# When layer 1's weight sums are made, and the order of the plain heads on two engines

## The chip, the core and the metric

The kernel runs on one core of a Trainium2 chip. The metric is the device time of one execution in microseconds (us). The kernel before was run three times: median 1727.48 us, from 1726.52 to 1728.12.

## The reference

Two layers over 512 prompt positions and 64 sample positions, all in float32 (D = 1024, 8 heads, feed-forward width 4096). Each layer:

```python
h = rmsnorm(x, g_pre_mix)
z = h @ w_in                       # [B | C | xin | c_q | c_kv | k_rope | gate_conv | gate_mla]
y_a = B * short_conv(C * xin)      # causal, 3 taps, with the last two rows kept
y_b = mla_attention(...)           # latent attention, chunk-causal mask, rotary key; the
                                   # sample attends to 512 cached positions and its own
merged = sigmoid(gate_conv) * y_a + sigmoid(gate_mla) * y_b
x = x + rmsnorm(merged @ w_o, g_post_mix)
f = square(relu(rmsnorm(x, g_pre_ffn) @ w1)) @ w2
x = x + rmsnorm(f, g_post_ffn)
```

The outputs are the two x, and for each layer the new latents, rotary keys and convolution rows.

## The kernel before, in words

**Arithmetic.** Every product of two float32 matrices is made of three products of fp32r matrices: each operand is split in a high part (a cast by ScalarE, `..._hi`) and a low part (a subtraction by VectorE, `..._lo`), and TensorE adds low x high, high x low and high x high in one PSUM bank (`mm3`, lines 811 to 813). So each weight block (128 x 1024, 512 KB) is loaded by SP into a slot, cast by ScalarE, subtracted by VectorE, and only then multiplied. Columns are worked on in two halves of 288 positions. Results of 288 columns go through a ring of four PSUM banks (`ring`), whose banks ScalarE and VectorE free by reading them (`ring_full`, `ring_free`); four more banks (`att`) serve attention and the second matrix of the feed-forward.

**Order.** All five instruction streams are written out by hand, each engine in its own order, with semaphores between them. SP issues nearly all loads, each after a wait for the product that last used the slot (`ring_full`, `w2_full`). An engine that waits holds up all that stands behind it in its stream.

**Stages of a layer.** First the latents' projection. Then eight heads. Heads 0, 1 and 7 are plain: five blocks (the two gates, C, xin, B), with the query, key and value projections, the scores, the turning of the probabilities and the product of probabilities and values between them. TensorE's order in a plain head is: block 0, projections, block 1, scores, block 2, turns, block 3, `attended` (probabilities x values), block 4. Heads 2 to 6 are mixed: two pairs of blocks each are multiplied by seven half products instead of eight, with sums and differences of the weight blocks (`weight_sums`) and of the inputs (`turn`). Then the output projection with the sample's attention in it, and the feed-forward in eight groups. Groups 0 and 1 are plain; groups 2 to 7 use the same seven products for two pairs of blocks (p = 0, 1) each. In their steady part TensorE alternates between a pair's seven ring products and eight banks of the second matrix (`w2_blocks`, 4 `att` banks in turn). I call one such pair with its eight banks a half group.

**The weight sums of the mixed heads.** There are 20, ten for each layer (2 for each of 5 mixed heads; `N_SUMS` = 20, `MIXED` = 5). GpSimd makes them in DRAM, by DMAs alone: three copies (`sums_copy`, lines 1129 to 1131, 1 MB), two accumulating DMAs (`sums_add_first`, 1135 and 1136), and two more (`sums_add_second`, 1139; `sums_add_third`, 1142), 256 KB each. `sums_steps` runs them as a pipeline: in step n it waits for the landing of what came before, copies sum n + 1, and adds to sums n, n - 1 and n - 2. The first two steps run before layer 0's key rotation (also on GpSimd), all others right behind it, for both layers in one go. SP loads the finished sums for the mixed heads (line 949 for 512 KB, 954 for halves) after waiting for `sums_third`. In the feed-forward's pairs the sums are made in SBUF by VectorE instead (`pair_sums`, lines 3009 to 3014), after it has waited for the landing of both blocks of the pair.

**A plain head on the two engines.** In ScalarE's stream (line 1501 on) the exponents are followed by `next_weight(2)` (the cast of a block of the next head), `small_hi(L, h + 1)` (the cast of the next head's small weights, which waits for their DMA) and `turned_hi(h)` (the casts of the turned probabilities, line 1494). VectorE has `next_weight(2)`, for head 1 `head_mix(3)` (2477), `turned_lo(h)`, `small_lo(h + 1)`, then the convolution: `u` from the banks of block 3 (2567 to 2570), ScalarE's `conv_begin`, `conv_taps`, the gate product, a weight, `attention_out` (2453, 2454), `gated_out` and `merge` (2355, 2363).

**Head 7** also prepares the sample's attention: casts of the transposed cache (`cth`, `kch`), copies of the new latents behind it, and the cache in natural order (`nah`, line 1567), with VectorE's `cache_lo(0)`, `(1)`, `(2)`. Right behind head 7 stands the output projection: `merged_lo` (2744) gives the low parts of the eight merged rows; rows 0 to 6 come back from DRAM, row 7 is head 7's own. TensorE starts it with rows 0 to 3 of output columns 0 to 3, then `s_scores(0)`, rows 4 to 7, and `s_turn(0)` (3663), which needs the sample's softmax (2777).

**The feed-forward's loads.** SP loads a pair's first block when product 1 of the pair before is done, its second after product 4 (`after_pair`, `pair_load`), and the blocks of the second matrix after the banks that used the slot (`after_w2`). VectorE's order for a half group (`outs_and_lo`) is: `pair_sums`, then the reads of the second matrix's banks (`w2_out`, 2923) with the low parts of the next pair between them:

```python
pair_sums(g1, p1)
f_done(g0, p0, 2)
w2_out(g, k0)
f_done(g0, p0, 3)
w2_out(g, k0 + 1)
```

## Time and profile before

| | before |
|---|---|
| median of 3 runs | 1727.48 us (1726.52 to 1728.12) |
| the profiled execution | 1726.3 us, its span 1724.5 us |
| TensorE busy | 1705.7 us (99%) |
| VectorE busy | 1309.3 us (76%) |
| ScalarE busy | 855.1 us (50%) |
| GpSimd busy | 122.3 us (7%) |
| granted TensorE clock, mean | 0.997 |
| SP's DMA queue | 185.45 MB, 33.5% of 16 engines |
| GpSimd's DMA queue | 41.95 MB, 13.8% of 16 engines |

The span runs from the first to the last instruction of the program; the profiled execution's own time has 1.8 us around it. Engines: PE is TensorE, PEld its weight loads, DVE VectorE, ACT ScalarE, POOL GpSimd, SP the queue that issues loads; a q behind an engine's name is its sequencer. L with a number is a line of the kernel. Most low parts are made in one helper, line 2071, so they are told apart by the tiles named. In a timeline's row the brackets at the end give the idle time of the engine before the instruction, and what ended it. Weight loads are `w_raw<-blocks_in`, issued at line 859 when a whole block is loaded.

### The profile page before, as it was taken

What the parts mean: (1) busy time and instruction counts of PE and PEld (TensorE: products, weight loads), DVE (VectorE), ACT (ScalarE), POOL (GpSimd) and SP (SyncE); (2) the same over time, 40 slices, a digit from 0 to 9 for tenths busy, and PEclk for the clock granted to TensorE, in tenths of its full rate; (3) what the DMA queues carried; (4) which work ended last, traced back from release to release, by engine and by line L of the source; (5) the groups of instructions that cost most, each with busy time, mean ns of one, the idle gap of its engine ahead of it and who ended that gap; (6) DMA issues with size and microseconds to landing.
All of it is one profiled execution on the core that took longest, in us unless ns stands there. A gap on an engine that the chain in (4) does not pass through costs nothing.

```text
span 1724.5 us, 31894 instructions
## 1 busy us (share of the span) xinstructions
PE 1705.7 (99%) x12735; PEld 1690.9 (98%) x12735; DVE 1309.3 (76%) x2514; ACT 855.1 (50%) x1665; POOL 122.3 (7%) x163
## 2 busy tenths in 40 slices
PE   9999999999999999999999999999999999999997
PEld 9998999999999999999999999999999999999997
DVE  7788787767798786668687797777678887777665
ACT  7625454545465454436366364545435536444452
POOL 1412121212210000000001000000000000000000
PEclk9999999999999999999999999999999999999998
DMA  7899898898762232323124454343532213322231
GB/s 239 198 212 244 214 209 211 178 249 235 163 129 97 89 96 86 99 86 111 60 84 149 148 166 139 114 121 112 171 117 98 99 37 111 98 86 87 74 99 55
DMA packets 90996, 231.54 MB, mean 134 GB/s; under 512 B 9824, under 2 KB 25440, under 8 KB 90848
## 3 DMA queue, kind: packets, MB, share of 16 engines
q1 hardware_dynamic: 71968, 185.45, 33.5%
q0 software_dynamic: 17600, 41.95, 13.8%
q8 instruction: 101, 1.65, 0.4%
q10 hardware_dynamic: 1280, 2.10, 0.3%
q14 instruction: 47, 0.39, 0.1%
HBM read 214.39 MB, written 57.02 MB: 157 GB/s over the span
## 4 chain that ended last, share of the span: by engine, by line
PE 94%; DMA 2%; DVE 2%; ACT 1%; SPq 1%; issue 0%; DVEq 0%; ACTq 0%
PE ring L811 19%; PE ring L813 19%; PE ring L812 19%; PE att L811 11%; PE att L813 11%; PE att L812 11%; PE att L3527 1%; DMA cache_pe_raw<-cache_pe_in 1%; PE att L806 1%; PE att L805 1%; DMA small_raw<-small_in 1%; DMA xs_lo_raw<-h_kept 1%; PE att L818 0%; ACT rope_s L1291 0%; PE att L3343 0%
## 5 line engine op out<-in xcount | busy, mean ns | idle before, releaser
L811 PE MATMUL ring<-xs_hi,w_lo 128*128 128x288 f32 x1872 | 556.6, 297 | 4.3 <-DVE xs_lo L2744 2.2
L813 PE MATMUL ring<-xs_hi,w_hi 128*128 128x288 f32 x1872 | 551.4, 295 | 0.0
L812 PE MATMUL ring<-xs_lo,w_hi 128*128 128x288 f32 x1872 | 551.3, 294 | 0.0
L2071 DVE TENSOR_TENSOR w_lo<-w_raw,w_hi 128x1024 fp32r<-128x1024 f32 (+1 forms) x364 | 370.0, 1035 | 37.3 <-ACT w_hi L1220 27.2
L811 PEld LDWEIGHTS ring<-xs_hi,w_lo 128*128 128x128 f32 x1872 | 351.6, 188 | 7.3 <-DVE ga L2355 2.4
L812 PEld LDWEIGHTS ring<-xs_lo,w_hi 128*128 128x128 f32 x1872 | 351.7, 188 | 1.4
L813 PEld LDWEIGHTS ring<-xs_hi,w_hi 128*128 128x128 f32 x1872 | 351.5, 188 | 0.0
L813 PE MATMUL att<-f_hi,w_hi 128*128 128x288 f32 x960 | 283.2, 295 | 0.0
L812 PE MATMUL att<-f_lo,w_hi 128*128 128x288 f32 x960 | 282.9, 295 | 0.0
L811 PE MATMUL att<-f_hi,w_lo 128*128 128x288 f32 x960 | 282.6, 294 | 0.0
L811 PEld LDWEIGHTS att<-f_hi,w_lo 128*128 128x128 f32 x960 | 180.4, 188 | 0.0
L812 PEld LDWEIGHTS att<-f_lo,w_hi 128*128 128x128 f32 x960 | 180.4, 188 | 0.0
L813 PEld LDWEIGHTS att<-f_hi,w_hi 128*128 128x128 f32 x960 | 180.4, 188 | 0.0
L1212 ACT ACTIVATE w_hi<-w_raw 128x1024 fp32r<-128x1024 f32 x98 | 101.9, 1053 | 87.0 <-DMA w_raw<-blocks_in 86.8
L1220 ACT ACTIVATE w_hi<-w_raw 128x1024 fp32r<-128x1024 f32 x118 | 122.8, 1051 | 7.2 <-DMA w_raw<-blocks_in 6.5
L2923 DVE TENSOR_TENSOR my<-att,my 128x288 f32<-128x288 f32 x160 | 70.8, 451 | 67.7 <-PE att L813 67.7
L813 PE MATMUL ring<-mix_hi,w_hi 128*128 128x288 f32 x384 | 113.5, 295 | 0.0
L811 PE MATMUL ring<-mix_hi,w_lo 128*128 128x288 f32 x384 | 113.1, 295 | 0.0
L812 PE MATMUL ring<-mix_lo,w_hi 128*128 128x288 f32 x360 | 105.9, 294 | 0.0
L811 PE MATMUL ring<-turn_hi,w_lo 128*128 128x288 f32 x320 | 94.9, 296 | 0.0
L812 PE MATMUL ring<-turn_lo,w_hi 128*128 128x288 f32 x320 | 94.4, 295 | 0.0
L813 PE MATMUL ring<-turn_hi,w_hi 128*128 128x288 f32 x320 | 94.2, 295 | 0.0
(342 smaller groups left out, 3184.4 us busy)
## 6 DMA issues: line engine op xcount, KB each, us to landing
w_raw<-blocks_in SPq DMA_DIRECT2D x195, 512.0 KB, 3.7
weight_sums<-blocks_in POOLq DMA_DIRECT2D x80, 256.0 KB, 7.2
w_raw<-blocks_in SPq DMA_DIRECT2D x62, 256.0 KB, 4.6
weight_sums<-blocks_in POOLq DMA_DIRECT2D x20, 512.0 KB, 5.6
weight_sums<-weight_sums POOLq DMA_DIRECT2D x40, 256.0 KB, 7.6
w_raw<-weight_sums SPq DMA_DIRECT2D x20, 512.0 KB, 4.6
w_raw<-weight_sums SPq DMA_DIRECT2D x40, 256.0 KB, 4.4
small_raw<-small_in SPq DMA_DIRECT2D x16, 320.0 KB, 4.6
```

Source lines behind the costliest of these rows:

```text
L805: pe.matmul(out, both, keys[1], start=False, stop=False)
L806: return pe.matmul(out, both, keys[0], start=False, stop=True)
L811: pe.matmul(out, w[1], x[0], start=first, stop=False)
L812: pe.matmul(out, w[0], x[1], start=False, stop=False)
L813: return pe.matmul(out, w[0], x[0], start=False, stop=last)
L1212: act.activation(hi, raw, ACT.Copy).then_inc(pl.weights_hi, 1)
L1220: act.activation(hi, raw, ACT.Copy).then_inc(pl.weights_hi, 1)
L2071: return dve.tensor_tensor(out, a, hi.bitcast(F32), ALU.subtract)
L2923: dve.tensor_tensor(dst, src, dst, ALU.add).then_inc(pl.w2_free, 1)
L3527: last = pe.transpose(att[:, to:to + P], pl.probs[:, PO[t] + P * j:PO[t] + P * (j + 1)], ident)
```

## The change

It has four parts. On GpSimd, `sums_steps` gets a first and an end sum, and layer 1's ten sums are made in a second run of the pipeline. That run starts after layer 0's are complete and the first product of pair (2, 1) of layer 0's feed-forward is full. In plain heads `turned_hi` goes ahead of `next_weight(2)` and `small_hi` on ScalarE, and `turned_lo` ahead of `next_weight(2)` on VectorE. In head 7 the copies of the new latents come after `conv_begin`, `cache_lo(1)` after the products into `u`, and the cast and subtraction of the natural cache go behind head 7, after the weight block `wo` 4. At the output projection `merged_lo` of rows 0 to 6 comes before head 7's `gated_out` and `merge`. No instruction is added or removed, but for the waits of the second run.

```diff
@@ -1141,24 +1141,24 @@
         def sums_add_third(n):
             pool.dma_start(pl.sums[n][:, 3, :], pl.sums[n][:, 0, :], accum_op=ALU.add).then_inc(pl.sums_third, 16)
 
-        def sums_steps(n0, n1):
+        def sums_steps(n0, n1, first, end):
 
             for n in range(n0, n1):
-                if n < N_SUMS:
+                if n < end:
                     pool.wait_ge(pl.sums_copied, 48 * (n + 1))
-                if 1 <= n <= N_SUMS:
+                if first < n <= end:
                     pool.wait_ge(pl.sums_first, 32 * n)
-                if 2 <= n <= N_SUMS + 1:
+                if first + 1 < n <= end + 1:
                     pool.wait_ge(pl.sums_second, 16 * (n - 1))
-                if n >= 3:
+                if n > first + 2:
                     pool.wait_ge(pl.sums_third, 16 * (n - 2))
-                if n + 1 < N_SUMS:
+                if n + 1 < end:
                     sums_copy(n + 1)
-                if n < N_SUMS:
+                if n < end:
                     sums_add_first(n)
-                if 1 <= n <= N_SUMS:
+                if first < n <= end:
                     sums_add_second(n - 1)
-                if n >= 2:
+                if n > first + 1:
                     sums_add_third(n - 2)
 
         pool.sem_inc(pl.ring_free, 4)
@@ -1186,13 +1186,17 @@
 
         pool.wait_ge(pl.x_landed[7], 16)
         sums_copy(0)
-        sums_steps(0, BEFORE_KEYS)
+        sums_steps(0, BEFORE_KEYS, 0, 2 * MIXED)
         for L in range(DEPTH):
             pool.wait_ge(pl.tables_landed, L * 32 + 32)
             key_rope(L, 0)
             key_rope(L, 1)
             if L == 0:
-                sums_steps(BEFORE_KEYS, N_SUMS + 2)
+                sums_steps(BEFORE_KEYS, 2 * MIXED + 2, 0, 2 * MIXED)
+                pool.wait_ge(pl.sums_third, 16 * 2 * MIXED)
+                pool.wait_ge(pl.ring_full, full(0, r_pair(2, 1, 0)))
+                sums_copy(2 * MIXED)
+                sums_steps(2 * MIXED, N_SUMS + 2, 2 * MIXED, N_SUMS)
         for i, (m0, m1) in enumerate(TAIL_MOVED):
             pool.wait_ge(pl.tail_factored, i + 1)
             nc.gpsimd.tensor_tensor(pl.x[:, m0:m1, cols(1)], pl.x[:, m0:m1, cols(1)], pl.last[:, m0:m1, :], ALU.add) \
@@ -1547,14 +1551,18 @@
                 next_weight(1)
                 absorbed_hi(h)
                 exponents(h)
+                turned_hi(h)
                 next_weight(2)
                 small_hi(L, h + 1)
-                turned_hi(h)
 
                 if h == HEADS - 1:
                     eng.wait_ge(pl.cache_landed, L * 48 + 48)
                     act.activation(pl.cth[:, :, 0:PAST], pl.ctraw[:, :, 0:PAST], ACT.Copy).then_inc(pl.cache_hi, 1)
                     act.activation(pl.kch[:, 0:PAST], pl.kcraw[:, 0:PAST], ACT.Copy).then_inc(pl.cache_hi, 1)
+                eng.wait_ge(pl.ring_free, ring_freed(3, 1))
+                apart()
+                conv_begin(h)
+                if h == HEADS - 1:
                     eng.wait_ge(pl.latent_lo, L * 4 + 4)
                     eng.wait_ge(pl.key_lo, L * 2 + 2)
                     apart()
@@ -1563,11 +1571,6 @@
                     for to, src in ((pl.kch, pl.keh), (pl.kcl, pl.kel)):
                         ins = act.activation(to[:, PAST:NT], src[:, NP_:NT].bitcast(F32), ACT.Copy)
                     ins.then_inc(pl.cache_new, 1)
-                    eng.wait_ge(pl.nat_landed, L * 16 + 16)
-                    act.activation(pl.nah[:, :, :], pl.naraw[:, :, :], ACT.Copy).then_inc(pl.cache_hi, 1)
-                eng.wait_ge(pl.ring_free, ring_freed(3, 1))
-                apart()
-                conv_begin(h)
                 next_weight(3)
                 if h == FIRST_MIXED - 1:
                     eng.wait_ge(pl.turn_made, 4 * (L + 1))
@@ -1665,6 +1668,8 @@
             for k in range(HEADS):
                 x_hi_a(k)
             weight_hi(L, n_wo(4), SLOT_WO[4], use_wo(4))
+            eng.wait_ge(pl.nat_landed, L * 16 + 16)
+            act.activation(pl.nah[:, :, :], pl.naraw[:, :, :], ACT.Copy).then_inc(pl.cache_hi, 1)
             eng.dma_start(conv_out[L], pl.conv_tail[:, :, :]).then_inc(pl.conv_stored, 16)
             eng.wait_ge(pl.new_turned, L + 1)
             act.activation(pl.n4h[:, :], pl.att[:, 1536:1792], ACT.Copy).then_inc(pl.cache_hi, 1)
@@ -2544,8 +2549,6 @@
                 if first:
                     pos_lo(L, 3)
                 head_out(h, pl.cv[:, cols(1)], 2, 1, pl.rx2)
-                if not first:
-                    next_weight(2)
                 if h == FIRST_MIXED - 1:
                     head_mix(3)
 
@@ -2553,13 +2556,11 @@
                 if first:
                     next_weight(0)
                     next_weight(1)
-                    next_weight(2)
+                next_weight(2)
                 small_lo(h + 1)
 
                 if h == HEADS - 1:
                     cache_lo(0, pl.ctl[:, :, 0:PAST], pl.ctraw[:, :, 0:PAST], pl.cth[:, :, 0:PAST])
-                    cache_lo(1, pl.kcl[:, 0:PAST], pl.kcraw[:, 0:PAST], pl.kch[:, 0:PAST])
-                    cache_lo(2, pl.nal[:, :, :], pl.naraw[:, :, :], pl.nah[:, :, :])
 
                 conv_state(h)
                 own_ring(h, 2, 1)
@@ -2569,6 +2570,8 @@
                 dve.tensor_tensor(pl.u[:, 2 + NH:2 + NP_], src[:, 0:NP_ - NH], pl.cv[:, NH:NP_], ALU.mult)
                 dve.tensor_tensor(pl.u[:, 4 + NP_:4 + NT], src[:, NP_ - NH:NH], pl.cv[:, NP_:NT], ALU.mult) \
                     .then_inc(pl.ring_free, 1)
+                if h == HEADS - 1:
+                    cache_lo(1, pl.kcl[:, 0:PAST], pl.kcraw[:, 0:PAST], pl.kch[:, 0:PAST])
                 conv_taps(h)
 
                 dve.scalar_tensor_tensor(out=pl.ga[:, 0:NP_], in0=pl.ga[:, 0:NP_], scalar=1.0,
@@ -2745,12 +2748,12 @@
                                          in1=pl.xh[:, m, t].bitcast(F32), op0=ALU.mult, op1=ALU.subtract) \
                     .then_inc(pl.x_lo, 1)
 
+            for k in range(HEADS - 1):
+                merged_lo(x_part(L, X_WOA + k), k, cols(0))
             k = HEADS - 1
             gated_out(k, 0)
             own_ring(k, 4, 0)
             merge(k, slice(0, NH), pl.merged_a)
-            for k in range(HEADS - 1):
-                merged_lo(x_part(L, X_WOA + k), k, cols(0))
             weight_lo(L, n_wo(3), SLOT_WO[3])
             k = HEADS - 1
             gated_out(k, 1)
@@ -2759,6 +2762,7 @@
             merge(k, slice(NH, NP_), pl.merged)
 
             weight_lo(L, n_wo(4), SLOT_WO[4])
+            cache_lo(2, pl.nal[:, :, :], pl.naraw[:, :, :], pl.nah[:, :, :])
             cache_lo(3, pl.n4l[:, :], pl.att[:, 1536:1792], pl.n4h[:, :])
             for k in range(HEADS):
                 merged_lo(x_part(L, X_WOB + k), k, slice(NH, NP_))
```

## Rows read from the trace of the kernel before

**Rows 1.** The page, part 1: busy us (share of the span) and instructions.

```profile
PE 1705.7 (99%) x12735; PEld 1690.9 (98%) x12735; DVE 1309.3 (76%) x2514; ACT 855.1 (50%) x1665; POOL 122.3 (7%) x163
```

**Rows 2.** TensorE's waits: what waited, releaser, us in total, times, longest.

```profile
PE att L811 <- DVE probs_t_lo L2071: 2.4, 1, 2.4
PE ring L811 <- DVE xs_lo L2744: 2.2, 1, 2.2
...
PE att L811 <- DVE k_lo L2071: 0.7, 1, 0.7
...
PE att L811 <- DVE rx L2454: 0.6, 1, 0.6
```

**Rows 3.** The timeline of GpSimd: start us, us, engine, line, operation; idle before it in brackets.

```profile
214.87 0.75 POOL L1129 DMA_DIRECT2D weight_sums<-blocks_in  x1 [7.08 <-DMA weight_sums<-weight_sums]
...
248.27 1.13 POOL L1139 DMA_DIRECT2D weight_sums<-weight_sums  x1
...
439.31 0.76 POOL L1129 DMA_DIRECT2D weight_sums<-blocks_in  x1 [4.42 <-DMA weight_sums<-weight_sums]
...
446.30 0.85 POOL L1136 DMA_DIRECT2D weight_sums<-blocks_in  x1 [4.28 <-issue]
...
453.64 0.81 POOL L1142 DMA_DIRECT2D weight_sums<-weight_sums  x1 [5.65 <-issue]
458.75 0.75 POOL L1129 DMA_DIRECT2D weight_sums<-blocks_in  x1 [4.30 <-DMA weight_sums<-weight_sums]
```

**Rows 4.** Busy us by stretch: PE, PEld, DVE, ACT, POOL, PEclk, DMA share, GB/s.

```profile
591.00:790.00 199.00, 199.00 (x1505) 199.00 (x1504) 142.91 (x266) 94.92 (x187) 0.00 (x0) 1.00 0.30 91
```

**Rows 5.** Timeline around head 1's turned probabilities, layer 0, three engines.

```profile
132.58 1.70 ACT L1228 ACTIVATE small_hi<-small_raw 128x1792 fp32r<-128x1792 f32 x1 [6.94 <-DMA small_raw<-small_in]
...
134.80 1.62 DVE L2071 TENSOR_TENSOR probs_t_lo<-att,probs_t_hi 128x512 fp32r<-128x512 f32 x3 [5.32 <-ACT probs_t_hi L1494]
...
136.47 0.50 PE L811 MATMUL att<-probs_t_hi,v_lo 128*128 128x512 f32 x1 [2.44 <-DVE probs_t_lo L2071]
```

**Rows 6.** Timeline of head 7 and the output projection, layer 0, VectorE and TensorE.

```profile
394.04 1.23 DVE L2071 TENSOR_TENSOR cache_n_lo<-cache_n_raw,cache_n_hi 128x1024 fp32r<-128x1024 f32 x1 [0.34 <-ACT cache_n_hi L1567]
...
401.94 0.46 DVE L2363 TENSOR_TENSOR my<-my,ga 128x288 f32<-128x288 f32 x1
402.32 2.66 DVE L2744 SCALAR_TENSOR_TENSOR xs_lo<-my,xs_hi 128x288 fp32r<-128x288 f32 x7
...
413.77 0.52 DVE L2777 TENSOR_SCALAR probs_s<-probs_s,stat_s 128x576 f32<-128x576 f32 x1
...
417.75 0.60 PE L3663 MATMUL att<-consts,probs_s 128*128 128x128 f32 x4
```

**Rows 7.** Timeline of ScalarE: it reads the first product of pair (2, 1).

```profile
590.97 0.39 ACT L1839 ACTIVATE pair_u<-ring 128x288 f32<-128x288 f32 x1
```

**Rows 8.** VectorE's block sums, 600 to 790 us: ns min/median/max, first and last start.

```profile
L3009 DVE TENSOR_TENSOR w_raw<-w_raw x8: 683/692/694, 613.1 to 778.9; 128x512 f32<-128x512 f32 x8
```

**Rows 9.** Weight loads of SP, 600 to 790 us: from issue to landing.

```profile
DMA to landing us min/median/max: 3.4/3.5/5.0
```

**Rows 10.** Timeline of one half group of the feed-forward, VectorE and TensorE.

```profile
683.56 0.69 DVE L3009 TENSOR_TENSOR w_raw<-w_raw 128x512 f32<-128x512 f32 x1
...
686.47 0.45 DVE L2923 TENSOR_TENSOR my<-att,my 128x288 f32<-128x288 f32 x1
...
689.27 0.30 PE L811 MATMUL att<-f_hi,w_lo 128*128 128x288 f32 x1
```

**Rows 11.** The same loads in layer 0's heads, 160 to 380 us.

```profile
DMA to landing us min/median/max: 3.6/7.9/11.3
```

**Rows 12.** DMAs issued from 249.0 to 249.9 us: count, KB, us to landing.

```profile
w_raw<-blocks_in SPq DMA_DIRECT2D x1, 512.0 KB, 8.4
weight_sums<-weight_sums POOLq DMA_DIRECT2D x1, 256.0 KB, 8.2
```

**Rows 13.** SP's loads of stored sums, 900 to 1100 us: first and last start.

```profile
L949 SPq DMA_DIRECT2D w_raw<-weight_sums x6: 320/324/339, 971.9 to 1088.1; - x6
```

## The prediction

> **What bounds the kernel now.** I read the page's busy times first [rows 1]: TensorE works 1705.7 of the 1724.5 us of the span, so everything that any reordering can win lies in the 18.8 us left, of which a part is start and end. The list of TensorE's own waits [rows 2] says where: 2.4 us in layer 0 before head 1's product of probabilities and values (it waits for the turned probabilities' low parts), 2.2 us in layer 0 before the output projection (it waits for the first low part of the merged rows), 0.6 and 0.7 us just behind the first of these, at head 2's keys and query. What is left is under 1 us each or belongs to the start and the end. Both large waits stand in layer 0 only; layer 1 runs the same code without them. What layer 0 has and layer 1 has not is GpSimd's traffic: the block sums of both layers are made by its DMAs, the twentieth copied at 458.75 us [rows 3]. From 591 to 790 us, in the feed-forward, TensorE has no idle time at all (199.00 of 199.00) and the DMA engines are 0.30 busy [rows 4]. So the change removes at most 2.4 + 2.2 = 4.6 us, and moves a load on the DMA engines into a stretch that has been free of waits. Hence the question is what that stretch can bear.
>
> **Head 1's turned probabilities.** ScalarE stood 6.94 us before the cast of the small weights, until their DMA landed at 132.6 us, and only then split the turned probabilities, which had long been there; VectorE waited 5.32 us with it, and TensorE came 2.44 us late at 136.47 [rows 5]. In the new order the split goes ahead of that wait and of one weight cast on each engine. VectorE is then free at 129.5 us (134.80 less its idle 5.32), its three subtractions take 1.62 us, so they are done near 131.1, ahead of 134.0, when TensorE asks. The 2.4 us go. What is late next: the small weights land as before, since no DMA of SP's queue moves. VectorE takes them at about 134.3 instead of 136.3, when its three subtractions ended: 2.0 us earlier, where TensorE comes 2.4 earlier; the wait of 0.6 us at head 2's keys, which hangs on VectorE, grows by 0.4. Behind it head 2 waits for rows reloaded by DMA. Those loads are issued when TensorE finishes a product, so they move up with it, but they queue behind GpSimd's transfers, which don't. That gives back between 0 and 2.0 us; I take 0.4, since TensorE's waits on that chain are 0.7 us and less. Saved: 2.4 - 0.4 - 0.4 = 1.6 us, with 0 and 2.4 as ends. Heads 0 and 7, and layer 1, have no such wait, so there the order is worth nothing, and the weight cast that now comes second has a whole head of cover: its block is multiplied in the next head.
>
> **Head 7.** In layer 0 the natural cache's subtraction (1.23 us) ran before the convolution, and behind it the weight, gating and merge steps of VectorE held the seven merged rows' subtractions back to 402.32 us; TensorE had then been ready since 400.7 [rows 2, 6]. The change takes the 1.23 us from in front, and puts the seven (2.66 us, so 0.38 each) before the gating and the merging (some 0.4 us each, [rows 6]) that only the eighth row needs. With 1.2 + 0.8 us out of the way the first low part is there at 402.32 + 0.38 - 2.0 = 400.7, just where TensorE asks: the 2.2 us go, with 1.4 as the low end if the high parts on ScalarE hold it. The moved cast and subtraction (1.05 us, as ScalarE's casts of this size, and 1.23) now precede the sample's first softmax: its normalisation ended at 414.29 and TensorE turned it at 417.75 [rows 6], so 3.4 us of cover for at most 2.3 us; without that cover it would cost up to 2.3. I take 0.
>
> **The sums, on the side that gets lighter.** Layer 0's ten end near 275 us instead of sharing the queue with the other ten until after 458. From there to 591 us the loads come faster, but TensorE waits there only before the output projection, counted already: 0.
>
> **The sums, on the side that gets heavier.** The new wait on GpSimd ends with the first product of group 2's second pair, read at 590.97 us [rows 7]. Ten copies lie between 214.87 and 458.75, 24.4 us each beside the heads' traffic, and the last two 19.4 apart [rows 3]; so the ten run from 591 to about 820 us. They meet eight half groups, from 613.1 to 778.9 us, counted by VectorE's block sums, 23.7 us apart [rows 8]. Nothing is queued behind the wait on GpSimd but the sums and the next layer's key rotation, some 80 us after they end.
> In each half group two weight blocks land just in time; loads of the stretch land in 3.5 us (3.4 to 5.0, [rows 9]). Upon the second one VectorE's block sum starts at 683.56, with no idle time before it, and behind it, in order, the first read of a second-matrix bank ends at 686.92; TensorE wants that bank at 689.27 [rows 10]. The spare is 2.35 us, so a landing time above 3.5 + 2.3 = 5.8 us stops TensorE by the excess.
> In layer 0's heads, beside the sums, such loads took 7.9 us in the median and up to 11.3 [rows 11]. One that met the sums almost alone, issued behind an accumulation of 248.27, took 8.4 us, and its GpSimd neighbour 8.2 [rows 3, 12]: a load seems to wait for what GpSimd has outstanding, and lands about 1.2 us behind it. With little else running, one cycle of the sums shows three waits of 7.0, 7.3 and 5.1 us (439.31, 446.30, 453.64, 458.75, [rows 3]). A load issued x us into a wait of T lands T - x + 1.2 us later and is too late by T - x - 4.6. Averaged over the cycle: (2.4^2 + 2.7^2 + 0.5^2) / 2 / 19.4 = 0.34 us per half group, 2.7 us for eight. The weight loads lengthen those waits by their own work, some 1.3 us each; then it is (3.7^2 + 4.0^2 + 1.8^2) / 2 / 23.3 = 0.70 us, 5.6 us for eight. These bound the likely case; I take 5.2, close to the second, since four loads in each half group meet the sums. Outer ends: 0 if the loads get their share at once, and 8 x (8.4 - 5.8) = 21 us if every one is hit like the one of rows 12.
> The Trainium skill, page "DMA: Bandwidth & Descriptors", section "Queues, rings and completion order", says that each DMA engine takes turns between the queues it has work for, packet by packet. By that alone a load would wait for one packet of GpSimd's and no more, and the term would be near 0 instead of 5.2. The row of 8.4 us speaks against it, though it is one load.
>
> **Sum.** -1.6 - 2.2 + 5.2 = +1.4 us on the profiled execution of 1726.3 us, which is 1.2 us below the median of the runs. On the median: 1727.5 + 1.4 = 1728.9 us.
>
> **Rivals.** All differ from the forecast in layer 0's feed-forward. A measurement of this kernel tells about 0.2%, 3.45 us, from no change.
> *Slower.* The collisions are worse than averaged: GpSimd's cycle (19.4 to 24.4 us) is nearly as long as a half group (23.7 us), so the phase hardly drifts, and a bad one repeats. With five of eight half groups late by 2.4 us it costs 12 us: 1727.5 - 3.8 + 12 = 1735.7 us. It decides from a mean lateness of 0.9 us per half group on ((3.45 + 3.8) / 8). For it: the 7.9 us in the heads, the zero slack in front of the block sum. Against it: the DMA engines have only 0.30 of other work here, and every stall shifts the phase.
> *Faster.* The loads get through: landing stays under 5.8 us, nothing is lost, and the time is 1727.5 - 3.8 = 1723.7 us. For it: the quickest of the heads' loads took 3.6 us with the sums running [rows 11]. Against it: the row of 8.4 us. The Trainium skill's rule of taking turns, named above, gives the same.
> *The sums come late for layer 1.* Its first load of a sum is at 971.9 us [rows 13], 150 us after they should be done; each would have to take some 37 us instead of 22. If so, TensorE waits tens of us there.
> *The change does not do what it says* for head 1: if the reloaded rows come no earlier, the whole 2.0 us is given back; the result is then 1.6 us above the forecast, inside its range.
>
> **How the numbers follow.** Forecast case 0.42: with a cost of 2.7 to 6.3 us and savings of 1.4 to 4.6 its own range is 1725.6 to 1732.4. Slower rival 0.35, faster rival 0.20, late sums 0.03. The cases reach from 1723 (all 4.6 us won) to 1735.5; late sums and more than five bad half groups are left out. The forecast case lies nearly all within 0.2%; so faster 0.20, same 0.42, slower 0.38.
>
> **What would show it.** Right: TensorE's list of waits without the 2.4 and the 2.2 us; new waits on the banks of the second matrix, released by VectorE, one to three us each, between 613 and 790 us, and a median landing above 5 us for the loads of that stretch; the wait at head 2's keys near 1.0 us. Wrong: no idle time of TensorE from 591 to 830 us (faster rival), a loss over 7 us there (slower rival), the 2.2 us still there before the output projection, or any new wait in layer 1.

## The result and the profile after

The changed kernel takes 1729.22 us in the median of 22 runs (1724.55 to 1734.16); the kernel before, run beside it on the same chip, 1725.05 us (22 runs, 1722.92 to 1730.66). The ratio is 1.0018, with a 95% interval of 1.0009 to 1.0026: slower by 3.1 us by the ratio (the two medians lie 4.2 us apart). The execution that was profiled is the longest of the 22, 1734.16 us (span 1732.4, where that of before was 1724.5), so its waits are to be read for their places and causes, and less for their sizes; sizes are taken below from the ratios too.

The page of the changed kernel, part 1 (as [rows 1]):

```profile
PE 1709.6 (99%) x12735; PEld 1693.3 (98%) x12735; DVE 1309.8 (76%) x2514; ACT 854.5 (49%) x1665; POOL 122.4 (7%) x163
```

TensorE's waits in the changed kernel (as [rows 2]: us in total, times, longest):

```profile
PE att L811 <- DVE my L2927: 8.7, 6, 2.6
PE ring L3367 <- DVE clear L2159: 1.5, 1, 1.5
PE att L811 <- DVE rx L2459: 1.3, 1, 1.3
```

The 2.4 us before head 1's product and the 2.2 us before the output projection are gone. In their place there are six waits for L2927 (it was L2923), VectorE's reading of a second-matrix bank. Their places, in TensorE's timeline:

```profile
615.36 0.41 PE L811 MATMUL att<-xs_hi,w_lo 128*128 128x288 f32 x1 [1.38 <-DVE my L2927]
...
713.92 0.40 PE L811 MATMUL att<-f_hi,w_lo 128*128 128x288 f32 x1 [2.43 <-DVE my L2927]
...
764.20 0.40 PE L811 MATMUL att<-f_hi,w_lo 128*128 128x288 f32 x1 [1.47 <-DVE my L2927]
...
790.93 0.40 PE L811 MATMUL att<-f_hi,w_lo 128*128 128x288 f32 x1 [2.63 <-DVE my L2927]
```

Five of the six lie in the stretch of [rows 4], and the sixth begins in it, at 788.3 us. It now reads (PE, PEld, DVE, ACT, POOL busy, clock, DMA share, GB/s):

```profile
591.00:790.00 199.00, 191.27 (x1434) 189.89 (x1432) 130.90 (x244) 89.47 (x176) 44.38 (x60) 1.00 0.83 185
```

and the weight loads of that stretch, 3.4/3.5/5.0 us in [rows 9], land after

```profile
DMA to landing us min/median/max: 3.5/5.8/9.3
```

The mechanism can be followed in one half group. The second block's load was issued at 778.79. The timeline of VectorE, GpSimd and TensorE, the same work as in [rows 10]:

```profile
784.66 0.81 POOL L1142 DMA_DIRECT2D weight_sums<-weight_sums  x1 [5.87 <-issue]
...
787.52 0.69 DVE L3013 TENSOR_TENSOR w_raw<-w_raw 128x512 f32<-128x512 f32 x1 [4.59 <-issue]
...
789.45 0.69 DVE L3018 TENSOR_TENSOR w_raw<-w_raw 128x512 f32<-128x512 f32 x1
790.06 0.45 DVE L2076 TENSOR_TENSOR f_lo<-ff,f_hi 128x288 fp32r<-128x288 f32 x1
...
790.42 0.45 DVE L2927 TENSOR_TENSOR my<-att,my 128x288 f32<-128x288 f32 x1
```

VectorE stood 4.59 us before the block sum, until the load was there, 8.7 us after its issue (the bracket names no releaser, but the landing at 787.5 us is the start of the block sum); the four block sums and one low part stand in its queue ahead of the bank read, and TensorE, whose last matmul had ended at 788.3, got its bank at 790.93.

Behind this longest wait something else follows. The windows of the changed kernel around it (columns as above):

```profile
787.80:791.20 3.40, 0.77 (x6) 0.54 (x5) 3.37 (x8) 3.15 (x6) 0.96 (x2) 1.00 0.16 27
791.20:794.60 3.40, 3.40 (x16) 3.40 (x16) 3.40 (x7) 1.07 (x2) 1.54 (x2) 0.51 0.77 72
794.60:798.00 3.40, 3.40 (x28) 3.40 (x26) 3.07 (x7) 0.00 (x0) 0.00 (x0) 0.99 0.88 146
```

TensorE is busy throughout the second window, but at a granted clock of 0.51, the 1.2 GHz level: 16 matmuls instead of 28. That cost some 1.6 us more. The shift of TensorE over the six waits themselves is 10.2 us, 0.25 us each more than the idle time. Both together are 3.1 of the 3.9 us by which the busy time of the page rose (1705.7 to 1709.6 us) with the same 12735 matmuls.

### The profile page after: what moved, and what is told of

It reads as the page before. It is cut to its first block, busy times and chain, and to the rows that moved or that the text cites. A ratio compares the mean times of both kernels' runs of the same rounds, so it can differ in the third digit from the quotient of the medians.

```text
span 1732.4 us, 31893 instructions
## 1 busy us (share of the span) xinstructions
PE 1709.6 (99%) x12735; PEld 1693.3 (98%) x12735; DVE 1309.8 (76%) x2514; ACT 854.5 (49%) x1665; POOL 122.4 (7%) x163
## 3 DMA queue, kind: packets, MB, share of 16 engines
q1 hardware_dynamic: 71968, 185.45, 33.1%
## 4 chain that ended last, share of the span: by engine, by line
PE 92%; DMA 4%; DVE 2%; ACT 1%; issue 1%; DVEq 0%; SPq 0%
PE ring L811 19%; PE ring L813 19%; PE ring L812 19%; PE att L811 10%; PE att L813 10%; PE att L812 10%; DMA w_raw<-blocks_in 2%; PE att L3531 1%; DMA xs_lo_raw<-h_kept 1%; PE att L806 1%; PE att L805 1%; PE att L818 0%; ACT rope_s L1295 0%; PE att L3347 0%; PE att L819 0%
## 5 line engine op out<-in xcount | busy, mean ns | idle before, releaser
L2927 DVE TENSOR_TENSOR my<-att,my 128x288 f32<-128x288 f32 x160 | 70.6, 452 | 56.3 <-PE att L813 56.2
```

The costliest lines, as they stand in the source:

```text
L2927: dve.tensor_tensor(dst, src, dst, ALU.add).then_inc(pl.w2_free, 1)
```

## The experiments

Twelve kernels, each beside the kernel before on the same chip. Since their profiles share every matmul, one table says where each gains and loses: the start of the same four matmuls (the one behind head 2's keys and query; the first of the output projection; the first after group 2's second pair was released; the first behind the feed-forward's eight half groups), and the span. The twelve were run in three sessions (e1 to e4; e5, e6, e7 and e9; e8 and e10 to e12), the changed kernel in one of its own, so any two of different sessions are compared through the kernel before.

```text
kernel             ratio, 95% interval      the same four matmuls start at     span
before             1                        170.14  402.92  591.12  795.03   1724.5
changed            1.0018 1.0009 to 1.0026  168.50  398.96  587.18  802.88   1732.4
e1 order only      0.9979 0.9969 to 0.9990  167.54  400.99  589.21  793.12   1721.9
e11 the same again 0.9987 0.9976 to 0.9999  168.30  400.57  589.08  792.99   1721.8
e7 turned only     1.0000 0.9990 to 1.0010  170.26  402.40  590.61  794.52   1724.2
e12 the same again 1.0000 0.9986 to 1.0015  169.16  401.71  591.47  795.38   1725.5
e8 head 7 only     0.9993 0.9981 to 1.0006  169.93  401.50  591.76  795.67   1725.1
e2 sums only       1.0025 1.0015 to 1.0035  169.63  399.80  588.02  800.48   1729.3
e3 no second run   0.9975 0.9963 to 0.9986  168.08  398.38  586.60  790.50   1719.3
e4 read first      1.0003 0.9992 to 1.0015  166.65  396.94  585.17  791.40   1721.4
e9 one at a time   1.0007 0.9995 to 1.0018  167.95  398.11  586.33  795.51   1724.4
e5 from head 7 on  0.9992 0.9981 to 1.0003  169.29  399.56  589.38  793.29   1722.1
e6 e5 and e4       0.9983 0.9974 to 0.9992  169.08  399.35  589.18  793.09   1722.0
e10 e5, e4 and e9  0.9990 0.9977 to 1.0003  167.85  398.05  588.31  792.31   1721.1
```

Each row of starts is one execution, and three things in it are no effect of an edit alone. Already near 125 us TensorE's starts differ by up to 0.9 us (124.3 to 125.2). A fall of the granted clock, of which the last section tells, costs 1.6 to 1.7 us where it happened (before the first start in e2, e7 and e8, behind the second in e12, behind the third in the changed kernel, e2 and e9). And the last 400 matmuls with the end take 62.2 us instead of 61.5 in the kernel before, the changed kernel, e8 and e12, where the lower clock at the end lasts 11.3 to 11.4 us instead of 7.7 to 9.3.

### The order alone, and the sums alone

e1_order_only is the changed kernel with the sums as before (the lines that matter; the conditions in `sums_steps` go back too):

```diff
-                sums_steps(BEFORE_KEYS, 2 * MIXED + 2, 0, 2 * MIXED)
-                pool.wait_ge(pl.sums_third, 16 * 2 * MIXED)
-                pool.wait_ge(pl.ring_full, full(0, r_pair(2, 1, 0)))
-                sums_copy(2 * MIXED)
-                sums_steps(2 * MIXED, N_SUMS + 2, 2 * MIXED, N_SUMS)
+                sums_steps(BEFORE_KEYS, N_SUMS + 2)
```

> The changed kernel with GpSimd's sums as before (all 20 in one go from layer 0's start), so only the order of the plain heads, head 7 and the output projection is changed. Theory (the loss lies in the late sums alone, the order gains): 3.8 to 4.2 us less than before, ratio about 0.9977; TensorE's list without the 2.4 and 2.2 us, with the wait at head 2's keys near 1.3 us, and no idle time from 591 to 860 us. Rival (the order loses part elsewhere, through the moved cast and subtraction of the natural cache or the traffic that is still there in head 7): the 2.2 us before the output projection stays or a new wait appears behind it, and the ratio is 0.9985 or above.

e2_sums_only is the kernel before with the opposite edit.

> The kernel before with only GpSimd's part of the change: layer 1's sums start at the feed-forward's pair (2, 1). Theory (weight loads land late behind GpSimd's transfers): waits of TensorE on the second matrix's banks, 5 to 11 us in sum between 600 and 800 us, while the 2.2 us before the output projection go, since head 7 is free of the sums' traffic, and the 2.4 us in head 1 stay: 3 to 8 us more than before, ratio 1.002 to 1.005. Rival (the bank waits come from the earlier arrival of TensorE that the new order brings): no bank waits here, ratio about 0.999.

e1 took 1723.26 us, 0.9979. Its feed-forward is the kernel before's again: 203.91 us between the last two matmuls of the table in both. e2 took 1730.54 us, 1.0025, and that stretch is 212.46 us long. So the loss is the sums', and the order is a gain. TensorE's waits in e2:

```profile
PE att L811 <- DVE my L2927: 5.8, 5, 2.2
PE att L811 <- DVE probs_t_lo L2075: 2.1, 1, 2.1
```

The surprise is in e1's list. Head 7's order is in it, and still:

```profile
PE ring L811 <- DVE xs_lo L2743: 1.9, 1, 1.9
```

while e2, without that order, has no such wait. The 2.2 us of [rows 2] therefore went with the traffic and not with the order. Beside the traffic of all twenty sums this wait is 2.2, 1.6 and 1.9 us without head 7's order (before, e7, e12) and 1.9, 1.7 and 1.1 us with it (e1, e11, e8). ScalarE's timeline in e1 shows how the order's gain is stopped:

```profile
395.36 1.06 ACT L1220 ACTIVATE w_hi<-w_raw 128x1024 fp32r<-128x1024 f32 x1 [2.48 <-DMA w_raw<-blocks_in]
398.89 1.06 ACT L1220 ACTIVATE w_hi<-w_raw 128x1024 fp32r<-128x1024 f32 x1 [2.47 <-DMA w_raw<-blocks_in]
399.85 2.43 ACT L1660 ACTIVATE xs_hi<-my 128x288 fp32r<-128x288 f32 x7
```

and VectorE's:

```profile
400.38 2.30 DVE L2743 SCALAR_TENSOR_TENSOR xs_lo<-my,xs_hi 128x288 fp32r<-128x288 f32 x6 [2.00 <-ACT xs_hi L1660]
```

VectorE is free at 398.4 now, against 402.32 before [rows 6], and then waits 2.00 us for the high parts, because ScalarE's weight cast stands ahead of them and its load is late. In the changed kernel the same load takes 3.6 us instead of 8.2 and is nearly on time, and the high parts come 4.0 us earlier:

```profile
394.38 1.06 ACT L1224 ACTIVATE w_hi<-w_raw 128x1024 fp32r<-128x1024 f32 x1 [0.46 <-DMA w_raw<-blocks_in]
395.82 2.45 ACT L1664 ACTIVATE xs_hi<-my 128x288 fp32r<-128x288 f32 x7 [0.38 <-PE ring L813]
```

The table has this for all: from its first to its second matmul, the kernels that have all twenty sums in the heads take 231.6 to 233.5 us (before, e1, e11, e7, e12, e8), and the eight that have ten take 230.2 to 230.5, e2 with the old order among them (230.17).

### No second run, and the bank read first

e3_no_second_run leaves out the making of layer 1's ten sums: layer 1's heads read layer 0's, so its values are wrong and only its time is of use.

```diff
-    return 2 * MIXED * L + 2 * (h - FIRST_MIXED) + c
+    return 2 * (h - FIRST_MIXED) + c
...
-                pool.wait_ge(pl.sums_third, 16 * 2 * MIXED)
-                pool.wait_ge(pl.ring_full, full(0, r_pair(2, 1, 0)))
-                sums_copy(2 * MIXED)
-                sums_steps(2 * MIXED, N_SUMS + 2, 2 * MIXED, N_SUMS)
```

> The changed kernel without layer 1's run of sums: layer 1's mixed heads read layer 0's stored sums, which leaves out the making of ten sums (the values of layer 1 are then not the reference's). Theory: all waits on the banks of the second matrix go, with nothing else changed; 3.8 to 4.2 us less than before, ratio about 0.9977, the same as with the order alone, and median landing of the loads from 600 to 790 us back at 3.5 us. Rival (the bank waits have another cause, such as the order on VectorE): they stay, and the ratio is 1.001 or above.

Measured 1721.76 us, 0.9975; landing is back at 3.6 us in the median and the stretch at 203.90 us. The difference to the changed kernel is the price of the second run in medians: 1.0018 - 0.9975 = 0.0043, 7.4 us (4.9 to 9.9 by the two intervals). What is left, 0.0025 or 4.3 us, is what the order and the lighter traffic win together.

e4_read_first leaves all transfers alone and takes the first of the four bank reads out from behind the block sums:

```diff
-                pair_sums(g1, p1)
                 f_done(g0, p0, 2)
                 w2_out(g, k0)
+                pair_sums(g1, p1)
                 f_done(g0, p0, 3)
                 w2_out(g, k0 + 1)
```

> The changed kernel, but in every half group of the feed-forward VectorE reads the first bank of the second matrix before the block sums instead of behind them. The loads and GpSimd are left as they are. Theory (TensorE waits because a bank's read is queued behind a block sum that waits for a late weight block): the spare before the second bank counts now, so each bank wait shrinks by about 1.5 us; the six waits of 8.7 us in sum in the changed kernel's profile become 2 us or so, and the time falls 5 to 7 us below the changed kernel's own profile, ratio to before 0.998 to 1.000. Rival (TensorE waits for late weights or for slower matmuls as such): the sum of its waits stays at 7 us or more.

Its loads of 600 to 790 us land no sooner than the changed kernel's:

```profile
DMA to landing us min/median/max: 3.6/6.7/9.0
```

but of TensorE's waits for the bank reads there is left

```profile
PE att L811 <- DVE my L2927: 1.1, 3, 0.7
```

and in its timeline VectorE reads the bank before the load is there, which still comes late:

```profile
776.50 0.46 DVE L2927 TENSOR_TENSOR my<-att,my 128x288 f32<-128x288 f32 x1 [0.39 <-PE att L813]
...
778.25 0.69 DVE L3013 TENSOR_TENSOR w_raw<-w_raw 128x512 f32<-128x512 f32 x1 [1.29 <-DMA w_raw<-blocks_in]
```

So in these traces it is the place of the read behind the block sum that turned late loads into idle time. The medians show less of it. The ratio is 1.0003, 0.0015 below the changed kernel's (0.0001 to 0.0029 by the two intervals, so 2.6 us and hardly clear of noise), where its waits (8.7 to 1.1 us) had promised 0.004; and it lies 0.0028, 4.8 us (2.1 to 7.6), above e3's, so the larger part of the second run's price may still be there. The two traces also lie at opposite ends: the changed kernel's is its slowest run, e4's its fastest (1723.21 beside a median of 1726.35), and even there the stretch takes 206.23 us against e3's 203.90. Where the rest is lost stays open.

### Fewer transfers outstanding

e9_one_at_a_time changes only the second run:

```diff
-                sums_steps(2 * MIXED, N_SUMS + 2, 2 * MIXED, N_SUMS)
+                for n in range(2 * MIXED, N_SUMS):
+                    pool.wait_ge(pl.sums_copied, 48 * (n + 1))
+                    sums_add_first(n)
+                    pool.wait_ge(pl.sums_first, 32 * (n + 1))
+                    sums_add_second(n)
+                    pool.wait_ge(pl.sums_second, 16 * (n + 1))
+                    sums_add_third(n)
+                    pool.wait_ge(pl.sums_third, 16 * (n + 1))
+                    if n + 1 < N_SUMS:
+                        sums_copy(n + 1)
```

> The changed kernel, but in its second run each of layer 1's ten sums is made step by step, one step's transfers waited for before the next is issued: same bytes, fewer of them outstanding together. Theory (a load lands behind what GpSimd has outstanding): weight loads from 600 to 790 us land sooner, median 4.5 us instead of 5.8, and the bank waits fall from 8.7 us to below 4; ratio 1.000. Rival (the landing goes by the bytes moved, or engines take turns between queues and the accumulations slow every packet): median at 5.5 us or more and bank waits of 6 us or more; ratio 1.001 to 1.003.

Landing and TensorE's waits in e9:

```profile
DMA to landing us min/median/max: 3.5/4.6/9.0
```

```profile
PE att L811 <- DVE my L2936: 3.1, 3, 2.4
```

4.6 instead of 5.8 us and 3.1 instead of 8.7 us, as the theory had it, and the stretch takes 209.18 us, 1.6 of them through a fall of the clock. The ratio is 1.0007 (0.9995 to 1.0018), which can be told neither from the changed kernel's nor from no change. The test isn't clean: the last third add comes at 864 us instead of 812, so the rate fell too, and the DMA engines are 0.68 busy from 591 to 790 us instead of 0.83.

### An earlier start

e5_start_at_head7, and e6_head7_read_first, which has e4's edit too:

```diff
-                pool.wait_ge(pl.ring_full, full(0, r_pair(2, 1, 0)))
+                pool.wait_ge(pl.ring_full, full(0, r_hd(HEADS - 1, 4, 1)))
```

> The changed kernel, but layer 1's sums start with head 7's last product (about 415 us) instead of group 2's. Theory (a load waits for what GpSimd has outstanding, and only the half groups after each other's second bank read have no more than 2.3 us to spare): the ten run from 415 to about 640 us and meet the half groups of 556, 577, 590, 613 and 636 us only; idle time of TensorE behind the second matrix's banks falls from 8.7 us to 2 to 4, none after 660 us, ratio 0.999 to 1.000. Rival (the bytes cost what they cost wherever they lie): idle time of 6 us or more between 400 and 660 us, ratio 1.001 or more.

> Both edits together: sums from head 7 on, and the first bank of the second matrix read ahead of VectorE's block sum. Theory: no idle time over 0.7 us from 400 to 860 us, ratio 0.9975 to 0.9985, at or below the order alone (0.9979), since the 1.9 us before the output projection is also gone. Rival: reading first only helped by chance of phase, and bank waits of over 1 us stand at the half groups of 556 to 636 us; ratio 0.999 or more.

e5 gives 0.9992 and e6 0.9983. From 591 us on both keep the kernel before's 203.91 us although GpSimd issues its last add at 631 us (the first copy at 400, not at the 415 expected), and e5 has no wait for a bank read at all, though its landing is 7.8 us in the median from 400 to 600 us. What they pay instead lies between the output projection and the table's third matmul: 189.8 us instead of 188.2, in e6 with a new wait of 1.3 us at 525.1. e6 beats the kernel before and the changed one, but it can't be told from e5 (0.0009 apart, each known to about 0.001). e10_all_three adds e9's loop to it:

> The changed kernel with three edits: layer 1's sums start at head 7, are made one step at a time, and the first bank of the second matrix is read ahead of the block sum. Theory (outstanding transfers make the landing, the spare makes the wait): ten sums from 415 to about 690 us, landing of the loads from 400 to 600 us 5 to 6 us in the median instead of 8.0, no idle time over 1 us from 400 to 860 us, ratio 0.9975 to 0.9983, as low as without the second run (0.9975). Rival (the rest of the loss isn't in waits behind banks): ratio 0.9985 or more, as without the third edit or worse, since the sums now meet more half groups.

It gives 0.9990; the loads of 400 to 600 us land in 7.1 us instead of 8.0, and TensorE has a wait of 1.8 us at 524.3. The expectation of 0.9975 to 0.9983 fell, and e10 can't be told from e6: nothing shows that making the sums one at a time adds to the early start.

### The order's two halves

e7_turned_only and e12_turned_again, the kernel before with the split of the turned probabilities ahead of the weight and the small weights, on ScalarE and likewise on VectorE:

```diff
                 exponents(h)
+                turned_hi(h)
                 next_weight(2)
                 small_hi(L, h + 1)
-                turned_hi(h)
```

> The kernel before with one edit: the turned probabilities are split before the head's third weight cast and the small weights' on both engines. Theory: the 2.4 us before head 1's product go and come back in part at head 2's keys and query (0.8 and 1.0 us), so 1.6 to 2.0 us are won; the 2.2 us before the output projection stand as before; ratio 0.9985 to 0.9992. Rival (the 1.9 us that the order alone left before the output projection show that only this edit is worth anything): ratio 0.9979, the same as with head 7's order.

> The turned order alone once more (1.000 the first time). Theory that what is won at head 1 comes back at head 2's keys and query, in a part that the DMA phase sets: between 1.9 and 3.5 us there, ratio 0.9985 to 1.000. Rival (it is worth as much as both orders together): 0.998.

e8_head7_only is the order without that edit; e11_order_again repeats e1.

> The kernel before with head 7's order alone (both engines), the turned probabilities split as before. Theory (the edits add up; the turned order was measured at 1.000 and both at 0.9979, so head 7's order carries what is won): ratio 0.998, the wait before the output projection gone or below 1 us, the 2.4 us at head 1 still there and in some runs followed by the lower clock. Rival (the wait before the output projection belongs to GpSimd's traffic in head 7 and not to the order, since it stood at 1.9 us with the order alone): a wait of 1.5 us or more there, ratio 0.9995 to 1.0005, and the order's 0.9979 was partly chance of phase.

> The order alone once more (the kernel that gave 0.9979 beside the kernel before), beside its two halves. Theory: 0.998 again, TensorE's waits at head 2's keys and query about 1.9 us together and no lower clock behind any of them. Rival (phase): 0.9990 or more, with waits of 3 us or more there.

The turned order alone gives 1.0000 twice. TensorE's waits in e7:

```profile
PE att L811 <- DVE k_lo L2071: 2.2, 1, 2.2
...
PE att L811 <- DVE rx L2454: 1.4, 1, 1.4
```

The 2.4 us are gone, and head 2's query and keys (in this order in the list) wait 3.5 us instead of 1.3: all but 0.25 us is given back by the waits, and the clock that fell behind the longer of them takes the rest. The forecast of 0.9985 to 0.9992 for e7 fell.

Head 7's order alone gives 0.9993, where 0.998 was expected. The wait before the output projection is between what theory and rival had said, and here it isn't the weight block that is late but the sample's cache, earlier in ScalarE's stream:

```profile
PE ring L811 <- DVE xs_lo L2745: 1.1, 1, 1.1
```

```profile
392.39 1.06 ACT L1556 ACTIVATE cache_t_hi<-cache_t_raw 128x1024 fp32r<-128x1024 f32 x1 [3.18 <-DMA cache_pe_raw<-cache_pe_in]
```

VectorE waits for this cast and comes to the merged rows at 400.90 us, after their high parts. So in e1, e11 and e8 most of what the order saves on VectorE is used up by a late load, and not always by the same one.

Both orders together give 0.9979 and 0.9987. None of the halves can be told from no change alone; together they can. How the gain divides between them these intervals do not settle. e11's waits at head 2's keys and query are 2.3 us together, where 1.9 was expected, and its 0.9987 beside e1's 0.9979 suggests, within the noise, that e1 was a little lucky.

## Why the prediction came out right, and where its steps were off

Forecast 1728.9 us, +1.4 on 1727.5; measured 1729.22, but +4.2 on a median of before that 22 runs put at 1725.05 where three had given 1727.48. By the ratio the change costs 3.1 us (1.6 to 4.5), which is 0.18% and so within the 0.2% that the forecast case was given. The sign, the place and the mechanism were forecast; the near agreement of the absolute times owes 2.4 us to the reference having been high.

**Head 1, -1.6 us: the size held as a mean, the reason only in part.** In the profiled run the matmul behind head 2's query starts 1.64 us earlier. Over the eleven kernels with the turned order it starts at 168.4 us in the mean, 1.5 us before the mean of the three without it (169.9), but from 166.65 to 170.26. The give-back was put at 0.4 + 0.4 us on the chain of these two waits. In the changed kernel they give back 0.1 us (1.35 + 0.12 beside 0.62 + 0.71); TensorE is 2.4 us ahead at head 1's product and 2.35 at head 2's query, and loses 0.7 us only between 160 and 170 us (0.23 of them in a wait for ScalarE). So the total is nearly the one forecast and the place is not. In e7 the two waits give back 2.2 us and a fall of the clock the rest. The case that the change would do nothing for head 1 was given as a rival; e7's trace is that case.

**Head 7, -2.2 us: right size, wrong cause.** In the profiled run the stretch up to the output projection is 2.3 us shorter. But this was booked on the order ("the 2.2 us go") while the lighter queue was booked at 0 because "TensorE waits there only before the output projection, counted already". e1 and e2 show the reverse. The order frees VectorE, as worked out; the step that failed is that the high parts on ScalarE were only kept as an end of the range, and they stand behind a weight cast that waits for a load. The sums' traffic sets when that load lands: 4.0 to 8.2 us after its issue in the six kernels that have all twenty sums in the heads, 3.6 to 3.8 in the other eight. A wait may be removed by either of two parts of a change, and booking it once is right for the sum but says nothing on which part earned it.

**The moved natural-cache steps, 0:** no wait appears at the sample's softmax in the changed kernel. Right there, though not always: e8, with the same order, waits 1.0 us at this place.

**The sums in the feed-forward, +5.2 us: right mechanism, too small.** The waits are where they were forecast, released by the instruction forecast, 0.2 to 2.6 us each, and the median landing crosses 5 us. The size is 7.4 us in medians (4.9 to 9.9), above the 2.7 to 6.3 of the forecast case, and in the profiled run 215.70 - 203.91 = 11.8 us. This term is the step that was mis-sized. The averaging took one load per half group and idle time alone. No run shows its 1.3 us for the weight loads' own work; by the table of the kernel before, SP's queue needs 1.6 us of all engines for 512 KB (185.45 MB in 33.5% of 1724.5 us), and with that the second average would have been 0.80 us per half group, 6.4 for eight. The upper bound of 6.3 us was given without a working. What the averaging missed besides: a wait puts a quarter of a microsecond on top of itself, and one of over 2 us may bring the lower clock for 1.6 us. The outer end of 21 us was never near.
The Trainium skill's rule of taking turns (page "DMA: Bandwidth & Descriptors", section "Queues, rings and completion order") had been read as a term near 0. That reading is refuted: the loads of this stretch land in 5.8 us in the median instead of 3.5, and 9 of the 29 that were issued between 600 and 790 us took over 7.0 us, twice what they take alone. Turns halve a load's share while both queues have work, and that alone, as an estimate, doubles 3.5 to 7.0 us; what goes beyond it no run here explains, and e9, where rate and depth changed together, does not decide between turns and waiting behind what is outstanding.

**Rivals.** The slower rival's condition, a loss of over 7 us in this stretch, holds in the profiled run and is about where the median stands (7.4 us beside the 7.25 from which it decides). The intervals don't decide between it and the forecast case. In the total it was held off by savings of 4.3 us, 0.5 more than forecast. The faster rival is out by e2 and e3. Late sums: layer 1 has no new wait, and the second run issued its last add at 812 us.

## What to carry to other kernels

A background transfer is priced by the spare time of the foreground loads it meets, and that spare is often not in the transfer but in what stands behind it in an engine's order: moving one 0.45 us read ahead of work that waits for a load took TensorE's waits for those reads from 8.7 to 1.1 us in the profiles, without touching a transfer (in the medians it won 2.6 us, hardly clear of noise, out of 7.4, so the spare in the order is not all of the price). Before moving traffic into a stretch because it has no idle time, look for the instruction there that waits for a load with results queued behind it. And when a change has an order part and a traffic part, run each alone: here the mixture was slower, while the order alone was faster by 0.13 to 0.21%, and the wait which the order was meant to remove went with the traffic.

## What the runs showed of the hardware that was not expected

TensorE's granted clock fell to the 1.2 GHz level for 3.4 us at the end of some short waits in the middle of the kernel; the fall began between 0.4 us before and 0.4 us after TensorE took up work again. In the fourteen profiles this happened seven times, behind waits of 1.89, 2.05, 2.08, 2.16, 2.25, 2.40 and 2.63 us (the last in the changed kernel; two in e2, one each in e7, e8, e9 and e12). It did not happen behind waits of 2.04, 2.21, 2.43 and 2.44 us, nor behind any of 1.87 us and less. Two windows of e2, behind waits of 2.08 and 2.04 us:

```profile
136.40:139.80 3.40, 3.40 (x15) 3.21 (x14) 2.37 (x7) 0.97 (x3) 2.71 (x4) 0.50 0.84 247
714.12:717.50 3.38, 3.38 (x25) 3.38 (x26) 3.38 (x7) 0.00 (x0) 0.82 (x1) 1.00 1.03 130
```

and of the kernel before, behind its 2.44 us:

```profile
136.47:139.90 3.43, 3.43 (x23) 3.30 (x24) 2.75 (x6) 0.56 (x2) 2.71 (x4) 1.00 0.69 227
```

So with the same length of wait it may happen or not, and each time costs about 1.7 us, half of 3.4 (1.6 us as measured in the changed kernel). It goes with a part of the spread from run to run: of 103 runs of the kernel before, the 25 with a mean clock of 0.998 have a median of 1724.3 us, and the 36 with 0.996 or less one of 1729.2. Those 4.8 us are more than one such fall. The mean clock also holds the lower stretch at the kernel's end, which lasts 7.7 to 11.4 us in the fourteen profiles and alone moves the mean by 0.001 and the time by 0.7 us. Whether longer waits bring the lower clock or both have a common cause is not tested. For this kernel it means that a wait of about 2 us cost some 1.1 us more than its length on average (7 falls of 1.7 us in 11 waits of 1.89 us and more), and that one trace of a kernel with waits near 2 us may lie several microseconds off its median.
